# 42 instead of 32 tokens of a second tile by gathered rows, and three instead of four first-matrix chunks between the routing of two heads

## What is computed

```
q = (a @ w_q).reshape(B, S, PEER_HEADS, PEER_QDIM)            # 8 heads
t1, i1 = lax.top_k(s1, 16);  t2, i2 = lax.top_k(s2, 16)       # scores against k1 and k2
top, sel = lax.top_k(t1[..., :, None] + t2[..., None, :], 16) # over the 256 pairs
gates = softmax(top);  experts = i1 * 128 + i2 of the chosen pairs
u_sel = u_exp[experts];  h = u_sel . a                        # 16384 x 2048 table
w = gates * gelu(h)
out = sum over 8 x 16 picks of w * v_exp[experts]             # 16384 x 2048 table
```

## Time and profile before

| | us |
|---|---|
| median of 3 runs | 3002.78 (2994.18 to 3005.68) |
| profiled execution | 2995.07 |
| its span, first to last instruction | 2992.9 |
| PE / DVE / ACT / POOL busy | 2950.2 / 2220.2 / 1255.1 / 1435.3 |
| 798.01 MB by DMA, mean | 267 GB/s |

### The profile page before, as it was taken

How to read it: one execution, slowest core, us unless ns; L and a number is a source line. 1 busy time by engine, 2 the same in 40 slices (tenths; PEclk the granted TensorE clock), 3 DMA queues, 4 the chain that set the end, 5 groups by cost and what they waited for, 6 DMA issues and landing times. The chain is left out here.

```text
span 2992.9 us, 43288 instructions
## 1 busy us (share of the span) xinstructions
PE 2950.2 (99%) x16888; PEld 2771.6 (93%) x16888; DVE 2220.2 (74%) x2801; ACT 1255.1 (42%) x1818; POOL 1435.3 (48%) x813
## 2 busy tenths in 40 slices
PE   9999999999999999999999999999999999999998
PEld 7888668889999999999999999999999999999787
DVE  5465664578878777777777669888888888986445
ACT  5224542333333333333333334555555555554422
POOL 1010000008888888888888125665555667660000
PEclk9999999999999999999999999999999999999999
DMA  8462222235445599999999889999999999994222
GB/s 297 169 241 86 71 85 98 99 123 125 128 125 137 132 338 339 361 354 364 358 349 362 329 306 412 406 410 403 407 410 408 402 407 401 400 381 152 97 96 99
DMA packets 205172, 798.01 MB, mean 267 GB/s; under 512 B 68208, under 2 KB 121472, under 8 KB 128736
## 3 DMA queue, kind: packets, MB, share of 16 engines
q1 hardware_dynamic: 90768, 405.36, 36.2%
q0 software_dynamic: 95440, 367.63, 34.0%
q10 hardware_dynamic: 18816, 23.11, 2.2%
HBM read 745.46 MB, written 50.51 MB: 266 GB/s over the span
## 5 line engine op out<-in xcount | busy, mean ns | idle before, releaser
L1745 PE MATMUL ps<-aH,wH 128*128 128x352 f32 (+2 forms) x3088 | 1062.0, 344 | 6.9 <-DVE wL L1048 6.9
L1747 PE MATMUL ps<-aH,wL 128*128 128x352 f32 (+2 forms) x3088 | 1059.1, 343 | 0.0
L1746 PE MATMUL ps<-aL,wH 128*128 128x352 f32 (+2 forms) x3088 | 1059.0, 343 | 0.0
L1048 DVE TENSOR_TENSOR wL<-raw,wH 128x2048 fp32r<-128x2048 f32 x333 | 787.5, 2365 | 224.6 <-ACT wH L626 221.9
L540 POOL DMA_INDIRECT gates<-gates_r,idx_d x384 | 753.9, 1963 | 377.9 <-DVE gates_r L1463 243.0
L626 ACT ACTIVATE wH<-raw 128x2048 fp32r<-128x2048 f32 x333 | 636.8, 1912 | 677.2 <-PE ps L1747 581.2
L1745 PE MATMUL ps<-actH,wH 128*128 128x352 f32 x2048 | 662.2, 323 | 3.2 <-DVE wL L1048 3.2
L1747 PE MATMUL ps<-actH,wL 128*128 128x352 f32 x2048 | 661.9, 323 | 0.0
L1746 PE MATMUL ps<-actL,wH 128*128 128x352 f32 x2048 | 661.4, 323 | 0.0
L1745 PEld LDWEIGHTS ps<-aH,wH 128*128 128x128 f32 x3088 | 581.2, 188 | 47.8 <-DVE wL L1048 6.6
L1747 PEld LDWEIGHTS ps<-aH,wL 128*128 128x128 f32 x3088 | 580.9, 188 | 38.1
(11 more groups left out here) (273 smaller groups left out, 2433.2 us busy)
## 6 DMA issues: line engine op xcount, KB each, us to landing
raw<-s_pu SPq DMA_DIRECT2D x128, 1024.0 KB
raw<-s_pv SPq DMA_DIRECT2D x128, 1024.0 KB
gates<-zeros POOLq DMA_DIRECT2D x22, 1024.0 KB, 8.6
pre<-ut ACTq DMA_DIRECT2D x128, 176.0 KB
pre_in<-pre SPq DMA_DIRECT2D x128, 176.0 KB
gate_in<-gates SPq DMA_DIRECT2D x128, 176.0 KB
raw<-s_out SPq DMA_DIRECT2D x16, 1024.0 KB
raw<-s_pq SPq DMA_DIRECT2D x16, 1024.0 KB
```

What stands on the lines that cost most here:

```text
L1048: V.tensor_tensor(wL[parity][:, :], src[:, :], wH[parity][:, :].bitcast(F), ALU.subtract).then_inc(lo_ready, 1)
L1745: mm(out, wh, xh, start=start, stop=False, skip_group_check=skip_group_check)
L1746: mm(out, wh, xl, start=False, stop=False, skip_group_check=skip_group_check)
L1747: return mm(out, wl, xh, start=False, stop=stop, skip_group_check=skip_group_check)
```

## The change

BT goes from 32 to 42. With it TD, the dense columns, goes from 352 to 342, SETS from 4 to 3 (126 partitions in use, SPAN), and B_PICKS from 32 to 43 (three sets of 43, 43 and 42), so there are 171 picks instead of 160. HEAD_U goes from 4 to 3: the routing holds 24 chunks, 104 come after it, and the first pick stands at chunk 28. U_PICKS becomes 70 (66 in the 90 slots up to chunk 118, 4 late), so 101 picks run beside the 118 second-matrix slots. ADDS_FIRST becomes 132, and 252 additions take turns with gathers, four to one, over 63 gathers. As a head now has an odd number of slots, the buffers' parity alternates from head to head (`slot_at`, `chunk_at`). `sel` is formed later, at the first pick of the second tile, and the last sum takes two PSUM banks and two additions.

```diff
-BT = 32
+BT = 42
...
-B_PICKS = A_PICKS // SETS
+B_PICKS = -(-A_PICKS // SETS)
+SPAN = SETS * BT
...
-HEAD_U = 4
+HEAD_U = 3
 ROUTE_U = HEAD_U * HEADS
-ADDS_FIRST = 164
+ADDS_FIRST = 132
 FIRST_PICK, LAST_PICK = ROUTE_U + 4, KEYS - GROUP - 2
-U_PICKS, LATE = 64, 4
+U_PICKS, LATE = 70, 4
...
+def slot_at(b, j):
+
+    return ((2 + HEAD_U) * b + j) % 2
+
+
+def chunk_at(b, j):
+
+    return (HEAD_U * b + j) % 2
...
-            with sp.Fori(0, HEADS) as h:
-                load_head(h)
+            with sp.Fori(0, HEADS // 2) as i:
+                for b in range(2):
+                    load_head(2 * i + b, b)
...
+            nc.gpsimd.memset(idx_b[:, :], 0).then_inc(b_cleared, 1)
+            nc.gpsimd.memset(gates_b[:, :], 0.0).then_inc(b_cleared, 1)
...
-                act.dma_start(idx_b[dst, :], idx_e[at_b:P, src]).then_inc(b_loaded, 16)
-                act.dma_start(gates_b[dst, :], gates_r[at_b:P, NTD - 1, src]).then_inc(b_loaded, 16)
+                src = slice(i * B_PICKS, min((i + 1) * B_PICKS, A_PICKS))
+                n = src.stop - src.start
+                if i == 0:
+                    act.wait_ge(b_cleared, 2)
+                act.dma_start(idx_b[dst, 0:n], idx_e[at_b:P, src]).then_inc(b_loaded, 16)
+                act.dma_start(gates_b[dst, 0:n], gates_r[at_b:P, NTD - 1, src]).then_inc(b_loaded, 16)
...
-                r4 = b_rep[:, :, :].rearrange("p k (r t) -> p k r t", t=BT)
+                r4 = b_rep[:, :, 0:SPAN].rearrange("p k (r t) -> p k r t", t=BT)
+                if SPAN < P:
+                    st.did(V.tensor_scalar(b_rep[:, :, SPAN:P], hT[:, :, TD:TD + P - SPAN], 0.0, None, ALU.mult))
...
-                V.tensor_reduce(sel[:, :], ident[:, :].rearrange("p (r t) -> p t r", t=BT), AX, ALU.add).then_inc(sel_ready, 1)
...
                 if j == A_PICKS:
+                    dve.wait_ge(b_loaded, 32 * SETS)
+                    V.tensor_reduce(sel[:, :], ident[:, 0:SPAN].rearrange("p (r t) -> p t r", t=BT), AX, ALU.add).then_inc(sel_ready, 1)
...
-                scale_chunk(uc + 2, 0, at_n(4))
+                if HEAD_U > 3:
+                    scale_chunk(uc + 2, chunk_at(b, 2), at_n(4))
                 pair_more(h)
-                lo(n + 6, 0)
+                if HEAD_U > 3:
+                    lo(n + 6, slot_at(b, 6))
...
-                        V.tensor_tensor(hT[:, :, TD:TA], hT[:, :, TD:TA],
-                                        ps[:, BACK[0], 0:KD * BT].rearrange("p (k t) -> p k t", t=BT), ALU.add).then_inc(b_added, 1)
-                        dve.wait_ge(b_added, 1)
+                        for r in range(2):
+                            ks = slice(8 * r, 8 * r + 8)
+                            V.tensor_tensor(hT[:, ks, TD:TA], hT[:, ks, TD:TA],
+                                            ps[:, BACK[r], 0:8 * BT].rearrange("p (k t) -> p k t", t=BT), ALU.add).then_inc(b_added, 1)
+                        dve.wait_ge(b_added, 2)
...
-                        ins = mm(ps[:, BACK[0], k * BT:(k + 1) * BT], b_acc[:, k, :], sel[:, :], start=True, stop=True)
+                        ins = mm(ps[:, BACK[k // 8], k % 8 * BT:(k % 8 + 1) * BT], b_acc[:, k, :], sel[:, :], start=True, stop=True)
```

More of the change, by code:

```diff
@@ L253, in trunk_layer @@
     idx_b = at("idx_b", [B_PICKS], U32, C0 + 12 * KB + 576)
[L254 to L257, removed]
+    gates_b = at("gates_b", [B_PICKS], F, C0 + 12 * KB + 768)
+    dots_b = at("dots_b", [B_PICKS], F, C0 + 14 * KB + 1472)
+    pick_wb = at("pick_wb", [B_PICKS], F, C0 + 14 * KB + 1664)
+    sel = at("sel", [BT], F, C0 + 14 * KB + 864)
     identR = at("identR", [P], R, C0 + 13 * KB)
@@ L392, in _, with load_head @@
                     load(S0["out"] + 2 * i + j, stream["out"][2 * i + j, :, :], j)
-            def load_head(h):
+            def load_head(h, b):
                 n = S0["head"] + (2 + HEAD_U) * h
                 for s in range(2):
-                    load(n + s, stream["pq"][2 * h + s, :, :], s)
+                    load(n + s, stream["pq"][2 * h + s, :, :], slot_at(b, s))
                 for s in range(HEAD_U):
-                    load(n + 2 + s, stream["pu"][HEAD_U * h + s, :, :], s % 2)
-            with sp.Fori(0, HEADS) as h:
-                load_head(h)
+                    load(n + 2 + s, stream["pu"][HEAD_U * h + s, :, :], slot_at(b, 2 + s))
+            with sp.Fori(0, HEADS // 2) as i:
+                for b in range(2):
+                    load_head(2 * i + b, b)
             nu = S0["pu"] - ROUTE_U
@@ L856, in head @@
                 A(pqT[b][:, 1, :], ps[:, 1, :], ACT.Copy).then_inc(pq_copied, 1)
-                hi(n + 3, 1, at_n(1))
+                hi(n + 3, slot_at(b, 3), at_n(1))
                 for j in range(HEAD_U - 1):
-                    hi(n + 4 + j, j % 2, at_n(2 + j))
-                    gelu(HEAD_U * h + j, j % 2)
-                    store_chunk(HEAD_U * h + j, j % 2)
+                    hi(n + 4 + j, slot_at(b, 4 + j), at_n(2 + j))
+                    gelu(HEAD_U * h + j, chunk_at(b, j))
+                    store_chunk(HEAD_U * h + j, chunk_at(b, j))
             head(0, 0, 0, S0["head"], first=True)
@@ L1479, in spread_tokens @@
                                        .to_broadcast([P, KD, SETS, BT]), ALU.mult))
-                V.tensor_reduce(sel[:, :], ident[:, :].rearrange("p (r t) -> p t r", t=BT), AX, ALU.add).then_inc(sel_ready, 1)
                 st.settle()
-                r3 = b_rep[:, :, :].rearrange("p k (r t) -> p (k r) t", t=BT)
-                V.tensor_tensor(r3, r3, rstd[:, TD:TA].unsqueeze(1).to_broadcast([P, KD * SETS, BT]), ALU.mult).then_inc(rep_ready, 1)
+                V.tensor_tensor(r4, r4, rstd[:, TD:TA].unsqueeze(1).unsqueeze(2).to_broadcast([P, KD, SETS, BT]), ALU.mult).then_inc(rep_ready, 1)
             HS = 2 + HEAD_U
@@ L1492, in retrieve @@
                 if not first:
-                    scale_chunk(uc - 1, 1, at_n(-1))
-                lo(n + 1, 1)
+                    scale_chunk(uc - 1, chunk_at(b, -1), at_n(-1))
+                lo(n + 1, slot_at(b, 1))
                 if first:
@@ L1498, in retrieve @@
                     index_of(0)
[L1499 removed]
+                lo(n + 2, slot_at(b, 2))
                 if first:
@@ L2016, in head_slots @@
                         pe.wait_ge(pq_copied, 2 * h + s - 1)
-                    tile(n + s, s, s, waits=N_SC["ffn"] if first and s == 0 else None)
+                    tile(n + s, slot_at(b, s), s, waits=N_SC["ffn"] if first and s == 0 else None)
                     if first:
@@ L2020, in head_slots @@
                 scores(h, b, 0)
-                u_slot(n + 2, 0, HEAD_U * h, 0, first=first)
+                u_slot(n + 2, slot_at(b, 2), HEAD_U * h, chunk_at(b, 0), first=first)
                 scores(h, b, 1)
@@ L2031, in head_slots @@
                                 ins.then_inc(b_tok_done, 1)
-                    u_slot(n + 2 + s, s % 2, HEAD_U * h + s, s, first=first and s == 1)
+                    u_slot(n + 2 + s, slot_at(b, 2 + s), HEAD_U * h + s, chunk_at(b, s), first=first and s == 1)
             head_slots(0, 0, first=True)
```

30 lines of the change are left out of this document (15 added, 15 removed).

## The result

The changed kernel takes 3100.72 us (median of 4 runs, 3096.66 to 3108.52), the kernel before 2998.48 beside it: ratio 1.0342, 95% interval 1.0309 to 1.0374. That is 102 us slower where I had forecast 14 us faster. The profiled execution took 3096.66 us with a span of 3094.9.

The account below looks back on a forecast made before the run. The prediction took PE as the bound, with DMA, POOL and DVE just under it. Its terms, -51.2 + 2.7 + 0.4 - 1.5 + 0.5 + 12 + 23, gave -14 us: 2989 us by the median, range 2961 to 3016.

Parts of the forecast that it names:

- +12 for closer picks: First-matrix chunks with picks: schedule wants one per 10.18 us, POOL gives one in 10.52; loss taken as +12 us.
- Its other end: First-matrix chunks with picks: POOL's additions may lock onto a pick every 10.18 us, making the loss 0.
- PE's 51.2 us: Both expert matrices: ten columns fewer in 12,288 matmuls at 4.17 ns each save PE 51.2 us, the whole gain.
- Head 2, +2.7 us: Routing, head 2: the second tile's low part comes 13.4 us after the head's start, due at 10.9; +2.7 us once.
- 9.4 of 10.9 us: Routing, read from head 5: low part ends at 9.4 us, due at 10.9, so no PE waits in heads 3 to 7.
- 2.7 + 0.4: Head 2's late low part, +2.7 us, and DVE's lag meeting the last index work behind the last head, +0.4 us.
- The fourth rival: Order in a head doesn't fit: each of five later heads stalls some 2 us, +10 in all, 2999; chance 0.05.
- First dot, -1.5 us: First pick: the gather comes 3 to 4 us earlier against its dot, so PE's longest wait goes, -1.5 us.
- Second matrix, +23 us: 118 second-matrix slots: DMA at 415 GB/s makes a slot 7.70 us, 27 over PE's pace less 4 lent: +23 us.
- The gathers starve the second-matrix slots: Second-matrix slots: if 406 GB/s is DMA's ceiling, 47 us over PE's pace; slower, 3020; chance 0.19.
- within 0.5%: Whole kernel: outcome within 15 us, about what can be told from no change; chance 0.38.
- the third rival: Only DMA takes back: POOL's additions aren't held up by DVE, the 12 us falls away, 2977; chance 0.09.

Follow-up runs that it names:

- pad96: The changed kernel with the gates table at a pitch of 352 columns, so the third tile's additions take 96 rows again: 3027.4 us, ratio 1.0093.
- padpre: pad96 with the stored pre-activations also at a row pitch of 352 columns (1408 bytes instead of 1368): 3004.4 us, ratio 1.0006.
- narrow342: The kernel before with only TensorE's matmuls of both expert matrices cut from 352 to 342 columns: 2979.7 us, ratio 0.9932.

## Why the prediction was wrong, point by point

The step that failed is the one I did not price: additions "ahead of the first gather" and among the gathers at the durations of the earlier trace rows, though the third tile's row count changed from 96 to 86 and one such addition from 1.42 to 2.45 us. That is 73 of the 116 us between forecast and result. A second term put at nothing is the pitch of the stored rows, 23 us, a third the waits of heads 4 and 6 and a stall that did not go, together some 6 us. The rest are sizes.

- *POOL's additions.* Cost: 73 us (after 3100.7, pad96 3027.4). The forecast put this stage at +12 for closer picks. With both tables mended the loop stands 9.7 us over PE's pace in 64 of its 90 slots, so that term was about right. Its other end, that POOL locks onto the faster pace, did not come about.
- *Rows of 1368 bytes.* Cost: 23 us (pad96 to padpre). I had only the bytes in the sum, 0.350 MB instead of 0.360, and not the pitch. Why it costs stays open.
- *PE's 51.2 us.* The term was mis-sized: 12,288 x 2.2 ns = 27 us, 24 less. The slope between 256 and 352 columns was taken for the slope between 342 and 352.
- *Head 2, +2.7 us.* Measured 2.9 there. But I had excluded waits in heads 3 to 7 (9.4 of 10.9 us), and heads 4 and 6 did wait, 1.8 and 1.9 us. The reading that failed is head 5 taken for all five: in the kernel before, the low part of heads 4 and 6 ended 7.2 and 7.3 us after their first matmul, not 4.4, because DVE stood idle 3.2 us ahead of it for nothing that the profile shows. With 5.0 more it misses 10.9. Head 4 of the kernel before, whose first matmul starts at 816.07:

```profile
820.58 0.52 DVE L1472 TENSOR_TENSOR ut<-ps,rstd 128x352 f32<-128x352 f32 x1 [3.18 <-issue]
821.02 2.28 DVE L1048 TENSOR_TENSOR wL<-raw,wH 128x2048 fp32r<-128x2048 f32 x1
```

With 0.8 us behind the last head PE waits 7.4 us in all from 680 to 1012, where the kernel before has no such wait and the steps had 2.7 + 0.4. The fourth rival had the mechanism and was too big.

```profile
PE ps L1770 <- DVE wL L1065: 7.4, 4, 2.9
```

- *First dot, -1.5 us.* Wrong in sign. DVE sat idle 7.0 us for its row instead of 3.7, the low part behind it came late, and PE waited 4.5 us (the wait at 1027.23 above). In the kernel before, it had waited 1.0 there: the 1.5 us of the earlier trace rows stands at 1562, in the loop, so I took the wrong wait for this stall. The longer stall belongs to the 86-row additions ahead of the gather. In padpre the first dot did not wait at all; the low part behind it still began 3.6 us late for nothing that the profile shows, PE waited 1.2 us, and nothing was gained. narrow342, the old order with short slots, has such a stall too, 7.7 us of PE. The wait in the kernel before, and the dot of the changed kernel:

```profile
1076.85 0.43 PE L1745 MATMUL ps<-aH,wH 128*128 128x352 f32 x1 [1.05 <-DVE wL L1048]
```

```profile
1022.68 2.29 DVE L1575 SCALAR_TENSOR_TENSOR rows<-rows,ps 128x2048 f32<-128x2048 f32 x1 [7.01 <-DMA rows<-uv_rows,idx_s]
```

- *Second matrix, +23 us.* 415 GB/s in the window and 7.73 us a slot, where I had 415 and 7.70. Over PE's real 7.574 that is 118 x 0.156 = 18 us. PE's waits from 1880 to 2890 are all for low parts, as said, but sum to 13.6 us instead of 20; matmuls at the lower clock level behind them add some 3:

```profile
PE ps L1770 <- DVE wL L1065: 13.6, 13, 3.1
```

The account: -14 forecast, +73 additions, +23 pitch, +24 PE, +4 heads, +2 first dot, -5 second matrix, -2 loop: +105, and +102.2 was measured. Each median is good to some 3 us, so the small terms are not proven by this sum.

Of the rivals none was right. "The gathers starve the second-matrix slots" had the right sign for the wrong place: DMA did reach 415 there. The changed kernel without the two row effects (padpre) lies in "within 0.5%", 15 us from the 2989 forecast for it, and the miss in PE's term, 24 us, more than explains that.

## What to carry to other kernels

When a size changes, follow it into every DMA that is shaped by it: the row count of each indirect transfer (80, 96 and 128 were good here, 86 was not) and the pitch of each table in DRAM, beside the bytes. A padded table keeps both; 352 columns for 342 were worth 96 us here. And don't take PE's time per column from widths 96 apart for a cut of ten: measure the very width, since 338 columns were slower than 340.

## What the runs showed of the hardware

- An indirect addition of 86 rows of 4 bytes took POOL 2.45 us in its short form, of 96 rows 1.42, of 128 rows 1.54, and sent 602 packets of 8 bytes that the others don't send. 80 rows behave as 96.
- POOL's indirect additions are held up by what DVE does beside them. In the kernel before, 126 additions ran mostly beside a low part (both operands in SBUF) and took 0.91 us more than their short form on the mean, 59 beside the adding of a value row (the same) 0.68, 60 beside a dot (one operand in PSUM) 0.11, those beside the top-16 search (MAX8, MATCH_REPLACE, FIND_INDEX8) under 0.01. So the blocked time in the forecast is real, and the ground of the third rival is gone. This is a sorting of one execution; no run took the low parts away.
- Gapless fp32r matmuls (128 x 128 weights, clock 1.00): 352 columns 160.0 ns, 346 159.5, 342 157.8, 340 155.4, 338 159.9. The time isn't monotonic in the width.
- Gathers of 8-KB rows to the first 64 partitions, beside full ones and weight loads, brought the stage from 414 to 298 GB/s at nearly full share (1.02 to 0.96): half the rows were dearer than all.
- Stores of 1368 bytes to DRAM rows at a pitch of 1368 bytes instead of 1408 cost 18.5 us of the whole, 15.4 of them in a loop at the limit of DMA. The stores' packets took no longer; the packets of the weight loads beside them took 10% more. Rows at a pitch of 1416 bytes made those 3% dearer and cost nothing measurable where PE had slack.
- PE ran matmuls of 342 columns 0.285 us apart behind a wait of 4.54 us and 0.158 apart otherwise.
- DMA held 411 to 415 GB/s over windows of 150 and 300 us in the kernels that asked for more.
